# Norm factors of a two-branch decode layer: first root in token columns, second root applied at PSUM eviction of the up projection

## The reference

```python
def rmsnorm(x, w):
    xf = x.astype(jnp.float32)
    y = xf * lax.rsqrt(jnp.mean(xf * xf, axis=-1, keepdims=True) + EPS)
    return (y * w.astype(jnp.float32)).astype(x.dtype)
...
    mixed = (jax.nn.sigmoid(ga) * (o_a @ w_a) + jax.nn.sigmoid(gb) * (o_hg @ w_b)) @ w_o
    x1 = x + rmsnorm(mixed, ln2)
    ffn, new_conv = conv_ffn(rmsnorm(x1, ln3), conv_buf, w_up, cw, cb, w_dn)
    y = x1 + rmsnorm(ffn, ln4)
```

## Time and profile before

| | us |
|---|---|
| median of 3 runs | 2108.43 |
| lowest, highest | 2103.07, 2110.52 |
| the profiled execution | 2107.65 |
| its span, first to last instruction | 2105.8 |
| PE busy in the span | 2000.6 (95%) |
| DVE busy, ACT busy | 1039.7 (49%), 861.4 (41%) |

### The profile page before, as it was taken

The page is one execution under the profiler, slowest core; times in us unless marked ns, Lnnn a source line. Parts: engine busy times, 40 slices in busy tenths (PEclk is TensorE's granted clock), DMA queues, the critical chain, the costliest instruction groups (busy, mean ns, idle before and its releaser), DMA issues. The chain is left out here.

```text
span 2105.8 us, 34893 instructions
## 1 busy us (share of the span) xinstructions
PE 2000.6 (95%) x13539; PEld 1942.8 (92%) x13539; DVE 1039.7 (49%) x1564; ACT 861.4 (41%) x1270; POOL 142.1 (7%) x215
## 2 busy tenths in 40 slices
PE   5999999998999999999988999999999999999896
PEld 4999988898899999999986999999999999999895
DVE  3322453332466666554347555533555543455465
ACT  5331454332334434443335444422454432345443
POOL 2420200221000000100000000000000000000000
PEclk9999999999999999999998999999999999999998
DMA  7898534667455554667551555555555555555452
GB/s 205 198 271 207 139 100 111 179 170 237 124 134 151 141 150 127 190 191 209 154 157 41 155 144 151 148 142 157 141 158 140 155 144 144 155 145 154 115 143 86
DMA packets 534852, 324.60 MB, mean 154 GB/s; under 512 B 9169, under 2 KB 523650, under 8 KB 534008
## 3 DMA queue, kind: packets, MB, share of 16 engines
q1 hardware_dynamic: 517184, 272.12, 48.7%
q0 software_dynamic: 12304, 45.49, 7.2%
q10 hardware_dynamic: 5288, 5.94, 0.8%
HBM read 305.01 MB, written 22.04 MB: 155 GB/s over the span
## 5 line engine op out<-in xcount | busy, mean ns | idle before, releaser
L1051 DVE TENSOR_TENSOR wlo<-raw,whi 128x2048 fp32r<-128x2048 f32 x252 | 577.7, 2292 | 864.8 <-ACT whi L614 864.8
L1520 PE MATMUL ps<-hH,whi 128*128 128x320 f32 x2752 | 873.4, 317 | 13.8 <-DVE hL L1071 5.3
L1520 PE MATMUL ps<-hH,wlo 128*128 128x320 f32 x2752 | 855.4, 311 | 0.0
L1520 PE MATMUL ps<-hL,whi 128*128 128x320 f32 x2752 | 855.4, 311 | 0.0
L614 ACT ACTIVATE whi<-raw 128x2048 fp32r<-128x2048 f32 x253 | 484.0, 1913 | 689.8 <-PE ps L1520 614.1
L1520 PEld LDWEIGHTS ps<-hH,whi 128*128 128x128 f32 x2752 | 522.3, 190 | 27.7 <-issue 17.7
L1520 PEld LDWEIGHTS ps<-hL,whi 128*128 128x128 f32 x2752 | 522.3, 190 | 0.9
L1520 PEld LDWEIGHTS ps<-hH,wlo 128*128 128x128 f32 x2752 | 521.3, 189 | 0.0
L1520 PE MATMUL ps<-aH,whi 128*128 128x320 f32 x704 | 218.2, 310 | 2.7 <-DVE aL L1464 2.7
L1520 PE MATMUL ps<-aL,whi 128*128 128x320 f32 x704 | 217.8, 309 | 0.0
L1520 PE MATMUL ps<-aH,wlo 128*128 128x320 f32 x704 | 217.7, 309 | 0.0
(11 more groups left out here) (294 smaller groups left out, 1790.9 us busy)
## 6 DMA issues: line engine op xcount, KB each, us to landing
raw<-in_w_up SPq DMA_DIRECT2D x88, 1024.0 KB, 5.7
raw<-in_w_in SPq DMA_DIRECT2D x85, 1024.0 KB, 5.7
raw<-in_w_down SPq DMA_DIRECT2D x32, 1024.0 KB, 5.8
raw<-in_w_out SPq DMA_DIRECT2D x16, 1024.0 KB, 5.8
raw<-in_w_down SPq DMA_DIRECT2D x16, 768.0 KB, 5.0
w_buf<-in_cmp_w SPq DMA_DIRECT2D x32, 256.0 KB, 5.8
raw<-in_w_branch_a SPq DMA_DIRECT2D x16, 512.0 KB, 4.2
raw<-in_w_branch_b SPq DMA_DIRECT2D x16, 512.0 KB, 5.4
```

What stands on the lines that cost most here:

```text
L1051: TT(wlo[:, slot], raw[:, slot], whi[:, slot].bitcast(F32), ALU.subtract).then_inc(lo_ready, 1)
L1520: ins = pe.matmul(out, ww[:, slot, w, :], xx[:, k, :], start=(start and q == 0 and p_ == 0), stop=(stop and q == last and p_ == 2), skip_g ...
```

## The change

- **Squares first.** In the out projection ACT squares and scales before it splits the next weight, DVE adds the square before its split; the two splits of the last tile (of up tile 1) move behind the history copies on ACT, and between the residual's tiles on DVE.
- **First root in token columns.** Three products with one column of `mean_d` leave the mean of each token on a partition (`mean_tokens`); DVE and ACT form the root on 128 x 3 (`stat`), and three products with the identity spread it as rows in PSUM (`root_rows`, bank 2), from where DVE reads it. The last norm gets the same.
- **Second root at the eviction.** `hH` and `hL` are made from `x1` times the weight alone. The root `rsu` is multiplied in where DVE (no longer ACT) moves each up product from PSUM into `ue`. The squares' means are summed in bank 7 between the matmuls of the first up tile.
- **Two up tiles at once.** Of the 16 steps of up tile 1, eight stand between those of tile 0; the second pair goes to banks 5 and 6 so that it needn't wait for the eviction of the first.
- The residual is formed in groups of 1, 1, 2, 4, 4 and 4 tiles.

```diff
@@ ACT, out projection
-                    split_after(N_OUT + u, j, 2)
                     act.wait_ge(used, m + (N_OUT + 1))
...
                     act.activation(y1[:, ds(m, 1), :].rearrange("p o t -> p (o t)"), ps[:, u, 0:T], ACT.Identity,
                                    scale=ln[:, 1, ds(m, 1)]).then_inc(free[u], 1)
+                    if u == 0 or not isinstance(j, int) or j < KT // 2 - 1:
+                        split_after(N_OUT + u, j, 2)
@@ ACT, boundary
-            act.activation(rsb[:], rsb[:], ACT.Sqrt).then_inc(rstd_ok, 1)
-            for k in range(KT):
-                act.wait_ge(x_new, k + 1)
-                if k >= 2:
-                    act.wait_ge(x_add, k - 1)
-                act.activation(sq[:, k % 2, :], x1[:, k, :], ACT.Square).then_inc(x_sq, 1)
-            act.wait_ge(mean_v, 2)
-            act.activation(rsb[:], rsb[:], ACT.Sqrt).then_inc(rstd_ok, 1)
-            for k in range(KT):
-                act.wait_ge(h_new, k + 1)
-                act.activation(hH[:, k, :], y1[:, k, :], ACT.Copy).then_inc(h2h, 1)
+            act.activation(stat[:, 3:6], stat[:, 3:6], ACT.Sqrt).then_inc(rstd_ok, 1)
             for i in range(4):
...
+            split_after(N_OUT + KT - 1)
+            for k in range(KT):
+                act.wait_ge(x_new, arrived(k))
+                act.activation(hH[:, k, :], x1[:, k, :], ACT.Copy, scale=ln[:, 2, k:k + 1]).then_inc(h2h, 1)
+                if k >= 2:
+                    act.wait_ge(x_add, k - 1)
+                act.activation(sq[:, k % 2, :], x1[:, k, :], ACT.Square).then_inc(x_sq, 1)
@@ ACT, up tiles
-                            split_after(n0 + c, j, 4)
-                            act.wait_ge(used, j * 4 + (n0 + c + 1))
+                            if not later(i):
+                                if s == 0:
+                                    split_after(n0)
+                                    split_after(n0 + 1)
+                                    act.wait_ge(mean_v, 2)
+                                    act.activation(rsu[:], rsu[:], ACT.Sqrt).then_inc(rstd_ok, 1)
+                            else:
+                                split_after(n0 + c, j, 4)
                             act.wait_ge(u_hist, i * 2 + (s + 1))
-                            A.add(act.activation(ue[:, par, s, 2:2 + SEQ], ps[:, s, 0:SEQ], ACT.Copy))
...
@@ DVE, boundary (root_tokens, root_rows and h_low are new)
+                V.add(TS(stat[:, 3:5], ps[:, 2, 0:2], EPS, None, ALU.add))
+                V.add(TS(stat[0:SMP, 5:6], ps[0:SMP, 2, 2:3], EPS, None, ALU.add))
                 V.sync()
-                dve.reciprocal(rsb[:], rsb[:]).then_inc(mean_v, 1)
+                dve.reciprocal(stat[:, 3:6], stat[:, 3:6]).then_inc(mean_v, 1)
...
+            for k0, k1 in RES_GROUPS:
+                if k0 == 4:
+                    split_after(N_OUT + KT - 1)
+                V.add(TT(y1[:, k0:k1, :], y1[:, k0:k1, :], ps[:, 2:3, 0:T].to_broadcast([P, k1 - k0, T]), ALU.mult))
+                for k in range(done, k0):
+                    h_low(k)
+                done = k0
                 V.sync()
+                TT(x1[:, k0:k1, :], x1[:, k0:k1, :], y1[:, k0:k1, :], ALU.add).then_inc(x_new, 1)
@@ DVE, up tiles
-                            split_after(n0 + 2 * par + s, j, 4)
+                            if not later(i) and s == 0:
+                                root_rows()
+                                split_after(n0)
+                                dve.wait_ge(rstd_ok, 2)
+                            dve.wait_ge(used, j * 4 + (n0 + 2 * par + s + 1))
+                            bank = up_bank(i, s)
+                            V.add(TT(ue[:, par, s, 2:2 + SEQ], ps[:, bank, 0:SEQ], rsu[:, 0:SEQ], ALU.mult))
...
+                            if later(i):
+                                split_after(n0 + 2 * par + s, j, 4)
+                            elif s == 0:
+                                split_after(n0 + 1)
@@ PE, boundary
+                EARLY = (5, 7, 9, 10, 11, 13, 14, 15)
+                    for k in range(KT):
+                        pe.wait_ge(h2l, k + 1)
+                        first(k, k + 1, 0)
+                        if k in EARLY:
+                            first(EARLY.index(k), EARLY.index(k) + 1, 1)
+                        pe.wait_ge(x_sq, k + 1)
+                        product(ps[:, 7, 0:T], c_("mean_d"), sq[:, k % 2, :], start=(k == 0), stop=(k == KT - 1)
+                                ).then_inc(x_add, 1)
+                    first(len(EARLY), KT, 1)
+                    pe.wait_ge(hist_ok, 4)
+                    gemm(n0 + 2, n0 % 2, ps[:, up_bank(1, 0), 0:T], hH, hL, all16)
+                    pe.wait_ge(mean_v, 2)
+                    gemm(n0 + 3, (n0 + 1) % 2, ps[:, up_bank(1, 1), 0:T], hH, hL, all16)
```

More of the change, by code:

```diff
@@ L356, in layer, with arrived, up_bank @@
         S(n) for n in ("y_fin", "yt_ps", "yt_ok", "nc_ps", "nc_ok", "y_out", "copy_out"))
+    RES_GROUPS = ((0, 1), (1, 2), (2, 4), (4, 8), (8, 12), (12, 16))
+    def arrived(k):
+        return 1 + sum(k >= k1 for _, k1 in RES_GROUPS)
+    def up_bank(i, s):
+        return s + 5 if isinstance(i, int) and i == 1 else s
     w_in = a["w_in"][0]
@@ new lines, in root_rows, with h_low @@
+            def root_rows():
+                dve.wait_ge(x_add, KT)
+                TS(rsu[:], ps[:, 7, 0:T], EPS, None, ALU.add).then_inc(mean_e, 1)
+                dve.wait_ge(mean_e, 1)
+                dve.reciprocal(rsu[:], rsu[:]).then_inc(mean_v, 1)
+            def h_low(k):
+                dve.wait_ge(h2h, k + 1)
+                STT(hL[:, k, :], x1[:, k, :], ln[:, 2, k:k + 1], hH[:, k, :].bitcast(F32), ALU.mult, ALU.subtract
+                    ).then_inc(h2l, 1)
+            root_tokens(1)
@@ L1431, in _ @@
+            for k in range(done, KT):
+                h_low(k)
             dve.wait_ge(hist_ok, 4)
@@ L1928, in _ @@
                 ins.then_inc(hist_ps, 1)
-            pe.wait_ge(mean_v, 1)
-            for k in range(KT):
-                pe.wait_ge(x_sq, k + 1)
-                ins = product(ps[:, 2, 0:T], c_("mean_d"), sq[:, k % 2, :], start=(k == 0), stop=(k == KT - 1))
-                ins.then_inc(x_add, 1)
+            root_rows(1)
             n0, r0, i0 = N_FFN, R_FFN, 0
@@ L1939, in turn, with first @@
                         pe.wait_ge(free[s], i + r0 // 2)
-                        if part == 0 and s == 0 and not later(i):
-                            for k in range(KT):
-                                pe.wait_ge(h2l, k + 1)
-                                gemm(n0, n0 % 2, ps[:, 0, 0:T], hH, hL, all16[k:k + 1], wait=(k == 0),
-                                     done=(k == KT - 1), start=(k == 0), stop=(k == KT - 1))
-                        else:
-                            gemm(i * 2 + (n0 + s), (n0 + s) % 2, ps[:, s, 0:T], hH, hL, all16)
-                turns(pe, cnt, turn)
+                        gemm(i * 2 + (n0 + s), (n0 + s) % 2, ps[:, s, 0:T], hH, hL, all16)
+                def first(k0, k1, s):
+                    gemm(n0 + s, (n0 + s) % 2, ps[:, s, 0:T], hH, hL, all16[k0:k1], wait=(k0 == 0), done=(k1 == KT),
+                         start=(k0 == 0), stop=(k1 == KT))
+                EARLY = (5, 7, 9, 10, 11, 13, 14, 15)
+                if part == 0:
+                    for s in range(2):
+                        pe.wait_ge(free[s], r0 // 2)
+                    for k in range(KT):
[11 more added lines that the diff above has]
+                    gemm(n0 + 3, (n0 + 1) % 2, ps[:, up_bank(1, 1), 0:T], hH, hL, all16)
+                    with pe.Fori(2, cnt) as i:
+                        turn(i)
+                else:
+                    turns(pe, cnt, turn)
                 n0 += 2 * cnt
@@ L1975, in _ @@
             pe.wait_ge(d_add, KT)
[L1976 removed]
+            mean_tokens()
+            root_rows(3)
             pe.wait_ge(nc_ok, 5)
```

69 lines of the change are left out of this document (35 added, 34 removed).

## The result

The first comparison gave 2090.3 us (median of 4 runs, 2089.55 to 2093.8) against 2108.62 us (4 runs, 2103.07 to 2110.52), a ratio of 0.9918 (95% interval 0.9899 to 0.9938). The profiled execution is the slowest of the four, 2093.8 us.

The account below looks back on a forecast made before the run. PE was taken as the bound, busy for 95% of the span, with 35.8 us idle at the boundary and a shorter chain at the end. 2107.65 - 9.4 (boundary) - 1.4 (end) = 2096.85, so 2097 us; range 2091.5 to 2105.

Parts of the forecast that it names:

- the sum: Whole kernel: profiled time less the gains at the boundary and the end, 2107.65 - 9.4 - 1.4 = 2096.85, so 2097 us.
- Part 4: PE's steps 2 to 15: 18.5 us, 2.0 for the low clock, 0.9 for waits; last mean product ends at 1131.4.
- part 1: Out projection's end: with squares ahead of the weight split, the sum of squares is ready 3.7 us earlier, at 1097.25.
- part 2: First norm's root in token columns: ready at 1100.7, against a first use at 1105.67 before.
- Part 3: Residual, hH and hL on ScalarE and VectorE: PE has step 2 from 1110.0.
- part 5: Second norm's root to third up tile: starts at 1136.7 instead of 1146.10, 9.4 us gained, after a 1.8 us split wait.
- Part 7: Kernel's end, last norm's sum of squares to first use: 2.65 us instead of 4.06, 1.4 us gained.
- Part 6: Up stage: 88 tiles' evictions on VectorE, 0.43 + 0.22 us each, cost nothing, with 2.7 us to spare.
- rival (d): Up stage: VectorE becomes the bound, 0.3 us lost in each of 44 pairs, 13 us, 2110; chance 3%.
- Rival (a): Steps 0 to 15: PE's clock stays low, third tile 3.9 us later than before, about 2110.1; chance 4%.
- Rival (b): Interleaved steps: mean product keeps 0.82 us or clock returns at 1120; 2100 to 2101, both 2104; chance 14%.
- Rival (c): Second up pair: its cover breaks and the fifth tile waits, 1.6 us lost if 2 us longer, 2098.5; chance 8%.

Follow-up runs that it names:

- the repeat: The changed kernel measured again, unchanged: 2095.15 us (5 runs), ratio 0.9945 against the kernel before.
- the fill: The changed kernel with 37 unread products more on TensorE in its three waits at the boundary: 2091.67 us (5 runs), ratio 0.9937 against the kernel before.
- squares first: The kernel before with squares ahead of the weight splits in out tiles 0 to 14 alone: 2105.19 us, ratio 0.9993.
- paced loads: The kernel before with the residual's load in 8 pieces and the history's in 4, one for each finished out tile: 2097.48 us (7 runs), ratio 0.9953.
- the new end: The kernel before with only the last norm's root formed in token columns; no total given, 2.68 us at the end.

## Why the prediction was wrong, point by point

- **The step that failed is the sum**, "2107.65 - 9.4 - 1.4 = 2096.85". It takes all that stands ahead of the out projection's end as unchanged, and has no term for it. A term of 2 us was missing: the third `w_in` load, which is shorter with TensorE's longer program. PE's first product with `blocks` follows it, 132.22 us in the change, 134.46 before and 132.50 with the longer TensorE program. The out projection starts at 970.6 to 976.4 us in the twelve profiles of kernels built on the change, at 975.6 to 983.2 in the six of those built on the one before, and at 974.2 with the longer TensorE program. By the medians of the two groups that is 4 us, so of some 2 of them no run shows the cause.
- Of the 6.55 us between 2096.85 and the measured 2090.3 the profile shows 3.05, and 2.37 of these lie ahead of the out projection's end. The other 3.5 are the distance from the profiled execution, the slowest of the four, to their median.
- **A part of the boundary was taken as certain that varies.** Part 4 counted 2.0 us for the low clock. The runs showed 0 to 1.5: boundaries of 39.06 to 40.57 in the change and its equals, so a gain of 9.3 to 10.8 us.
- With these terms the gain is 2 + 9.3 to 10.8 + 0.8 to 1.4 = 12.1 to 14.2 us. The second measurement of the change allows that, 11.6 us (8.9 to 14.3, on another chip), and the interval of the first, 17.3 us (13.1 to 21.3), just reaches it. All nine runs of the change have a median of 2092.25, inside the range; the 37 of before that stand beside them and the other timed kernels have 2107.47. So the first four were also a low draw, and the range ended too near below: its lower end was set from "a boundary gain of 6 to 11 us and an end of 0.4 to 1.8" and the spread, with nothing for what the sum leaves out.
- **Parts 1 and 2** were right in time and wrong in worth. The sum of squares was there 1.05 us after the end, the root's first use at 5.12 instead of 4.45 since the clock fell during the transposes. Of the 3.7 us of part 1 2.0 to 3.4 remain at the third tile, and the token columns add 0.1 to 1.0 at the first use. By subtraction, most of the gain there comes from what the prediction did not price by itself: the second norm's mean and root run beside the up tiles and are no longer ahead of them. No run undid that alone.
- **Part 3** (step 2 at 13.75 after the end; 13.76) and **part 5** (third tile at 40.5; 40.55) hit the profiled execution partly by luck. The root was 0.67 us late there and the chain from it to step 2 as much shorter than forecast (8.64 us for 9.3); in the repeat and the fill step 2 is at 13.26 and 13.27 and the third tile at 39.1. The order of the chain and its waits are as forecast (the wait for `wlo` 1.8; 1.49). **Part 7** (2.65; 2.67 to 3.23) stands, with an experiment behind it.
- **Part 6** stands. VectorE's share rose to 65.73 of 100 with PE at 100.00, so rival (d) falls. The 128x256 eviction out of PSUM takes 423 ns, the operation of that size without PSUM 426. By the Trainium skill (VectorE: DVE Perf Modes, The TRN2 errata) an operation that reads PSUM has the longer fixed term, as an estimate from its figures by some 65 ns; no row here shows that.
- **Rival (a)** falls: the clock was back at about 1113.6 with waits of up to 0.9 us still to come. It did fall after short waits and small products, and in the repeat of the change twice. So the pattern of the Trainium skill (TensorE: Matmul & The Clock Gate, A second HAM failure mode) is there, but at 1.5 us at most. **Rival (b)** falls with it: at the full clock the steps without a part of tile 1 are 0.97 us apart, three matmuls and a mean product, so 0.53 for the latter as taken. **Rival (c)** is right in kind: the fifth tile's cover is thin, 0.37 us short once the third tile starts 1.5 us sooner.
- Some of its small sums are off, without weight for the result: part 2's terms give 1100.6 and not 1100.7, and with both rows as they stand 1102.5 at least and not 1102.3. In part 3 0.48 and 2.29 us give a fixed term of 0.15 and not 0.07. Part 7's worst case is a gain of 0.6 and not 0.4.

## What to carry to other kernels

Compare the stages that a change does not touch as carefully as the one it does: a difference of 2 us ahead of the first changed instruction is a term of the result, and a forecast should leave room for it. In a chain of three engines, price an edit at the chain's end, not where it is made: undoing part 1 cost 5.2 us at step 0, 3.0 at step 2 and 2.0 at the third tile against one execution of the change, and 3.4 there against another, since the split that made room had been put into the chain further on and the low clock fell elsewhere. And look for large side loads next to a weight stream: cutting two into pieces gave 9.9 us in the kernel before, nearly as much as the whole rearrangement.

## What the runs showed of the hardware

- With TensorE's program longer at its end, 1 MB loads at the kernel's start took less time: 15.8 to 16.0 us from issue to landing (median of the two issued between 34 and 52 us) in the kernel before, its repeat and its four variants (squares first, paced loads, the new end, a longer VectorE program), 13.8 to 14.0 in the twelve profiles built on the change and in the one of the kernel before with the longer TensorE program. What connects the two (where program and data come to lie in memory, say) was not tried and stays open.
- The granted clock fell to 0.50 at 1097 while PE was busy for the whole window, with 88-column transposes and small products; a wait of 1.05 us and six products of one column stood ahead of that. With wide products in the waits the clock stayed at 1.00 over the same transposes. In another execution of the same kernel the clock was 0.50, 1.00 and 0.50 again within the boundary:

```profile
1095.00:1096.00 1.00, 0.93 (x4) 0.52 (x3) 0.00 (x0) 1.00 (x3) 0.00 (x0) 0.50 0.00 0
1102.00:1103.00 1.00, 0.31 (x2) 0.00 (x0) 1.00 (x2) 0.54 (x2) 0.00 (x0) 1.00 0.00 0
1106.00:1107.00 1.00, 1.00 (x5) 0.80 (x4) 1.00 (x2) 0.39 (x1) 0.00 (x0) 0.50 1.18 321
```

- The loads on POOL's queue beside the weight stream (2.5 MB of residual, and the history) cost PE 4.7 us in one wait and about 6.5 us over the stage (119.3 to 112.8); in pieces behind finished tiles no wait for `wlo` was left in the stage.
